# Two interleaved column tiles in the second block's projection, experts adding straight into the stream, and a reordered choice stage

## The reference, cut to what matters

```python
def first_block(x, ...):
    ...                                      # modulation, two attentions, out projection
    h2 = rms_norm(x, g_ffn) * (1.0 + sc_m) + sh_m
    x = x + gt_m * expert_choice_ffn(h2, ...)
    return rms_norm(x, g_final)

def expert_choice_ffn(h, ...):
    aff = softmax(h @ w_router + b_router)
    gate, idx = top_k(transpose(aff), 128)   # 128 tokens for each of 16 experts
    ye = (silu(xe @ w_gate) * (xe @ w_up)) @ w_down      # xe = h[idx]
    return scatter_add(idx, ye * gate)

def second_block(x, ...):                    # twice:
    h  = rms_norm(x, g)  * (1 + sc) + sh     # 1024 tokens; the 256 of the context likewise
    qa, ka, va, ga, qb, kb, vb, gb, qn, kn, vn, gn = split_proj(h @ w_in[l])  # 3584 columns
    ...                                      # q and k: rms norm per head, rotation; 3 attentions
    x = x + gt * (concat([ya, yb, yn]) @ w_out[l])
```

## Time and profile before

| | us |
|---|---|
| median of 3 runs | 4779.21 (4777.91 to 4781.35) |
| the profiled execution | 4777.51 |
| its span in the trace | 4775.8 |
| around the span | 1.7 |

### The profile page before, as it was taken

One profiled execution on the slowest core, in us unless ns is written; L12 is line 12 of the kernel. 1 busy time (PEld: TensorE's weight loads), 2 busy tenths in 40 slices (PEclk: granted clock), 3 DMA queues, 4 the chain that ended last, 5 costly groups with the idle time before them and its releaser, 6 DMA issues. The chain is left out here.

```text
span 4775.8 us, 70956 instructions
## 1 busy us (share of the span) xinstructions
PE 3700.5 (77%) x24823; PEld 3010.7 (63%) x24823; DVE 2445.8 (51%) x4503; ACT 2213.4 (46%) x3911; POOL 914.9 (19%) x756
## 2 busy tenths in 40 slices
PE   3986786887369999378987869675878987869548
PEld 3974665666258888266776647554657776658436
DVE  2114454443468878576425535465585425546555
ACT  2215554751047777322226657554332226657452
POOL 0214000000026565044540000000034540000002
PEclk7988998998679999689998989897989999989889
DMA  6237413414969999422323242332222323232432
GB/s 247 77 111 229 98 41 75 107 41 161 275 252 392 398 394 363 138 71 84 102 79 74 79 89 58 82 93 73 95 88 71 105 91 73 80 78 59 99 99 85
DMA packets 328019, 633.36 MB, mean 133 GB/s; under 512 B 115172, under 2 KB 171396, under 8 KB 326628
## 3 DMA queue, kind: packets, MB, share of 16 engines
q1 hardware_dynamic: 292448, 510.46, 34.1%
q0 software_dynamic: 33760, 112.88, 7.6%
q10 hardware_dynamic: 1444, 5.30, 0.3%
HBM read 490.39 MB, written 138.17 MB: 132 GB/s over the span
## 5 line engine op out<-in xcount | busy, mean ns | idle before, releaser
L1932 PE MATMUL pr_ps<-pr_wH,hT_part 128*128 128x512 f32 (+1 forms) x1120 | 438.8, 392 | 0.0
L1692 ACT ACTIVATE ex_high<-ex_ring 128x2048 fp32r<-128x2048 f32 x192 | 368.7, 1920 | 95.2 <-PE ex_pg L1668 39.9
L1738 DVE TENSOR_TENSOR ex_ring_part<-ex_ring,ex_high 128x2048 fp32r<-128x2048 f32 x144 | 371.8, 2582 | 49.9 <-ACTq L1693 37.9
L1932 PE MATMUL pr_ps<-pr_wH,x_sb_part 128*128 128x512 f32 x896 | 368.5, 411 | 10.4 <-DVEq L2006 10.4
L1932 PE MATMUL pr_ps<-pr_ws_part,x_sb_part 128*128 128x512 f32 x896 | 360.3, 402 | 0.0
L1145 DVE TENSOR_REDUCE aa_nm<-aa_ps 128x1 f32<-128x1280 f32 (+1 forms) x144 | 197.7, 1373 | 303.4 <-PE aa_ps L1051 302.7
L1633 POOL TENSOR_TENSOR ex_ring_part<-ex_ring,ex_high 128x2048 fp32r<-128x2048 f32 x48 | 238.4, 4966 | 216.9 <-ACTq L1693 216.9
L1061 PE MATMUL aa_ps<-ident,aa_prob 128*128 128x128 f32 x1312 | 209.8, 294 | 59.9 <-ACTq L1181 58.6
L1177 ACT ACTIVATE aa_prob<-aa_ps,aa_nm 128x512 f32<-128x512 f32 (+2 forms) x272 | 210.9, 775 | 87.5 <-DVEq L1146 45.3
L1932 PEld LDWEIGHTS pr_ps<-pr_wH,hT_part 128*128 128x128 f32 x1120 | 219.3, 196 | 46.4
L1145 DVE TENSOR_REDUCE ab_nm<-ab_ps 128x1 f32<-128x1280 f32 (+1 forms) x108 | 148.3, 1373 | 194.5 <-PE ab_ps L1051 194.1
(11 more groups left out here) (364 smaller groups left out, 9202.4 us busy)
## 6 DMA issues: line engine op xcount, KB each, us to landing
ex_ring<-in_w_gate SPq DMA_DIRECT2D x64, 1024.0 KB, 9.7
ex_ring<-in_w_up SPq DMA_DIRECT2D x64, 1024.0 KB, 8.1
ex_ring<-in_w_down SPq DMA_DIRECT2D x64, 1024.0 KB, 7.9
z_d<-pr_zT POOLq DMA_DIRECT2D x120, 256.0 KB, 3.1
pr_ws<-in_w_in SPq DMA_DIRECT2D x14, 2048.0 KB, 9.3
mod_w<-in_w_ada SPq DMA_DIRECT2D x10, 2048.0 KB, 13.4
rt_mw<-in_w_ada SPq DMA_DIRECT2D x8, 2048.0 KB, 13.1
proj<-pr_raw POOLq DMA_DIRECT2D x54, 256.0 KB, 2.3
```

The costliest lines, as they stand in the source:

```text
L1692: scalar.activation(wH[:, c % HL].bitcast(F32R), w_sb[:, c % SL], ACT.Copy)
L1738: vector.tensor_tensor(w_part[:, c % SL].bitcast(F32R), w_sb[:, c % SL], wH[:, c % HL], ALU.subtract)
L1932: mm = tensor.matmul(ps[:, g % 4, c0:c1], x.bitcast(F32R), w[:, c % 2, kk, c0:c1].bitcast(F32R), start=kk == 0 and i == 0, stop=kk == KC - ...
```

## The change

It has six parts:

1. **Projection.** The column tiles are taken in the order 1, 0, 3, 2, 6, 4, 5, and two neighbours of that order alternate: the second half of the token tiles of one (`SHIFT` = 5) between the first half of the next. `LAG` goes from 2 to 3, the weight ring from 2 to 3 slots, the rings `raw` and `zT` shrink to 2. The gain is taken with one or two broadcast instructions instead of one over a stored row, and DVE takes the sums and the rest of one step one after the other.
2. **Norm.** The first three column tiles are loaded ahead, not two.
3. **Router.** `x_d` is written in the grid's order, with a DRAM pattern of 2 by 64 rows; `moe_d` and its zeros are gone.
4. **Choice.** The 8 reordering loads are gone; the 11 expert loads are issued as 4, 4 and 3, each group ahead of one of the last three modulation chunks.
5. **Experts and close.** The gate vector is loaded at the experts' start and multiplied in with L1762's successor; the DMA adds to `x_d`. The close stage loads `x_d` in 8 transfers, has no multiplication and addition, and works in two halves with a root each.
6. **Output, second block.** All 8 pieces of the weights are split first (`W0` = `KC`).

```diff
-            W0 = 2
+            W0 = KC if make_y else 2
...
-                    pool.dma_start(x_d[t * P:(t + 1) * P, :], x_sb[:, t * D:(t + 1) * D]).then_inc(kept, 16)
-                    pool.dma_start(moe_d[t * P:(t + 1) * P, :], zero[:, :]).then_inc(zeroed, 16)
+                    pool.dma_start(x_d.rearrange("(c r) d -> r c d", r=ROWS)[t * P // GRID:(t + 1) * P // GRID],
+                                   x_sb[:, t * D:(t + 1) * D]).then_inc(kept, 16)
...
-                for ci in range(TC):
-                    sp.dma_start(x_sb[ci * ROWS:(ci + 1) * ROWS, :].rearrange("p (t d) -> p t d", d=D), by_columns(x_d)[ci])\
-                        .then_inc(turned, 16)
+                def experts(c0, c1):
+                    for c, (m, e, s_) in list(enumerate(expert_chunks()))[c0:c1]:
+                        sp.dma_start(ring[:, c], expert_rows(m, e, s_)).then_inc(wl[c], 16)
...
-                    if i == MW:
-                        for c, (m, e, s_) in enumerate(expert_chunks()[0:EX_RING]):
-                            sp.dma_start(ring[:, c], expert_rows(m, e, s_)).then_inc(wl[c], 16)
                     if i >= MW:
+                        experts((i - MW) * 4, min((i - MW + 1) * 4, EX_RING))
                         sp.wait_ge(mod_ps, i - MW + 1)
...
-                    pool.indirect_dma_start(moe_d, bass.IndirectOffsetOnAxis(ap=to_c[:, e:e + 1], axis=0), y[:, :], None,
+                    pool.indirect_dma_start(x_d, bass.IndirectOffsetOnAxis(ap=to_c[:, e:e + 1], axis=0), y[:, :], None,
...
-                    vector.tensor_scalar(y[:, :], pd[:, :], gate_c[:, e:e + 1], None, ALU.mult)
+                    else:
+                        dve.wait_ge(gl, 16)
+                    vector.scalar_tensor_tensor(y[:, :], pd[:, :], gate_c[:, e:e + 1], gt, ALU.mult, ALU.mult)
...
+                for t in range(ST):
+                    sp.dma_start(x_sb[:, t * D:(t + 1) * D], x_d[t * P:(t + 1) * P, :]).then_inc(xl[t], 16)
...
-        N, LAG, RAW, ZR = 512, 2, 4, 3
+        N, LAG, RAW, ZR, WS = 512, 3, 2, 2, 3
...
-        steps = [(c, t) for c in tiles_c for t in range(ST2)]
+        places = [(0, t) for t in range(SHIFT)]
+        for i in range(NC):
+            for t in range(SHIFT, ST2):
+                places += [(i, t)] + ([(i + 1, t - SHIFT)] if i + 1 < NC else [])
+        steps = [(order[i], t) for i, t in places]
+        begin = [places.index((i, 0)) for i in range(NC)]
+        end = [places.index((i, ST2 - 1)) for i in range(NC)]
+
+        split_after = {}
+        for i in range(1, NC):
+            for kk in range(KC):
+                split_after.setdefault(max(begin[i] - KC - 1 + kk, 0), []).append((i, kk))
...
-                    vector.tensor_tensor(zq, zq, gain[:, ZC[c]:ZC[c] + w], ALU.mult)
+                    for m, (at, cs, _, _) in enumerate(gains):
+                        h0, h1 = (max(at, ZC[c]) - ZC[c]) // hd, (min(at + cs, ZC[c] + w) - ZC[c]) // hd
+                        if h0 < h1:
+                            vector.tensor_tensor(z3[:, h0:h1, :], z3[:, h0:h1, :],
+                                                 g1[:, m:m + 1, 0:hd].to_broadcast([P, h1 - h0, hd]), ALU.mult)
...
-                for q in range(len(qk) + 1):
...
+                for g in qk:
+                    sums(g)
+                    rest(g)
```

More of the change, by code:

```diff
@@ L1805, in _, with summed @@
             def _(act):
+                def summed(x, out_):
+                    scalar.activation(sqr[:, :], x, ACT.Square, accum_out=out_)
+                    act.drain()
                 for t in range(CT):
[L1807 to L1812, removed]
@@ L1813, in _ @@
-                act.drain().then_inc(sq, 1)
-                act.wait_ge(var, 1)
-                scalar.activation(rt[:, :], ss[:, :], ACT.Sqrt)
-                act.drain().then_inc(root, 1)
+                    summed(ctx_sb[:, t * D:(t + 1) * D], squares[:, ST + t:ST + t + 1])
+                for i, (t0, t1) in enumerate(halves_):
+                    for t in range(t0, t1):
+                        act.wait_ge(xl[t], 16)
+                        summed(x_sb[:, t * D:(t + 1) * D], ss[:, t:t + 1])
+                    act.drain().then_inc(sq, 1)
+                    act.wait_ge(var, i + 1)
+                    scalar.activation(rt[:, t0:t1], ss[:, t0:t1], ACT.Sqrt)
+                    act.drain().then_inc(root, 1)
@@ L1928, in _ @@
                             if t == 0:
[L1929 removed]
+                                pe.wait_ge(w_low if i else w_first, (i - 1) * KC + kk + 1 if i else kk + 1)
                             hH, hL = high_of(t)[:, kk * P:(kk + 1) * P], hT_part[:, kk, t * P:(t + 1) * P]
[L1931 to L1933 removed]
+                            for m, (x, w) in enumerate(((hH, wH), (hH, w_part), (hL, wH))):
+                                mm = tensor.matmul(ps[:, g % 4, c0:c1], x.bitcast(F32R), w[:, i % WS, kk, c0:c1].bitcast(F32R),
+                                                   start=kk == 0 and m == 0, stop=kk == KC - 1 and m == 2)
                         mm.then_inc(mm_done, 1)
@@ L1988, in _ @@
                         turned(g - LAG)
-                    if g < len(steps) and c + 1 < len(tiles_c) and 1 <= t <= KC:
-                        weights_high(c + 1, t - 1)
+                    for i, kk in split_after.get(g, ()):
+                        weights_high(i, kk)
             @block.vector
@@ L2007, in _ @@
                 dve.wait_ge(gl, 16 * 7)
-                for m, (at, cs, nm_, w) in enumerate(gains):
-                    scale = w ** -0.5 if "_q_" in nm_ else 1.0
-                    vector.tensor_scalar(gain[:, at:at + cs].rearrange("p (h d) -> p h d", d=w),
-                                         g1[:, m:m + 1, 0:w].to_broadcast([P, cs // w, w]), scale, None, ALU.mult)
+                for m, (_, _, nm_, w) in enumerate(gains):
+                    if "_q_" in nm_:
+                        vector.tensor_scalar(g1[:, m, 0:w], g1[:, m, 0:w], w ** -0.5, None, ALU.mult)
                 dve.drain()
@@ L2179, in first_block @@
             hT, hT_part = twins(held, "hT1", [P, KC, S])
-            ring, ahead = weight_ring(held, "p1", a["w_in"][0], IN1 // 6)
+            ring, ahead = weight_ring(held, "p1", a["w_in"][0], IN1 // 6, (0, 1))
             stage_norm("n1", [(x_sb, ST, 0, D, 0)], a["g_mix"], hT, ahead=ahead)
@@ L2241, in second_layer @@
             hT, hT_part = twins(held, f"hT2{l}", [P, KC, S2])
-            ring, ahead = weight_ring(held, f"pr{l}", a["w_in_2"][l], 512)
+            ring, ahead = weight_ring(held, f"pr{l}", a["w_in_2"][l], 512, COLUMN_TILES[0:3])
             stage_norm(f"n2{l}", [(x_sb, ST, 1, base + D, base), (ctx_sb, CT, 2, base + D, base)],
```

117 lines of the change are left out of this document (47 added, 70 removed).

## The result

The kernel after takes 4670.3 us in the median (4669.1 to 4670.9); before it was 4779.4. The ratio is 0.977 (95% interval 0.975 to 0.979): 109 us faster. Forecast were 4642.5, with 4570 to 4685 as the range. A stage is counted from the first instruction of its list to the first of the next one's; choice and experts begin here with their first working instruction, the first `max` and the first gather. The unchanged stages ahead of the router took 1.7 less in this execution; in the kernels of this study the router starts anywhere from 1137.0 to 1149.4.

A forecast was written before the change was run, and what follows sets the result against it. No engine bounds the whole; each stage ends by its own last arrival. Projection -120, norm +9, choice -44, router +50, close -15, output -15 make -135 against 4777.5: 4642.5 us, range 4570 to 4685.

The forecast's parts named there:

- Router: Router stage: dropping the zeros gains 5, but the reordered store to x_d costs more; 50 us more in sum (25 to 67).
- the upper bound: Router's x_d store: cut by its outermost count, two DMA engines carry 256 KB each, 10.5 us.
- The plain-store rival: Router: the reordered store costs no more than the plain one; -5 instead of +50, 4587.5 in all; chance 0.27.
- Projection, pace: Projection, first matmul to last step at PE's pace: 406 and 374 us, 60 and 78 less in layers 0 and 1.
- the 2.4 us that a pair leaves: Projection: DVE's slack in a pair of heavy and raw step, some 11.5 us on PE against DVE's 9.08.
- the hold on DVE and its price, 2.0: Projection: POOL's weight pieces may block DVE on a shared port pair; 2.0 again makes 11.1 of 11.5, the sum stays.
- 14.3 us a step: Projection: slower case, holds lengthen DVE's heavy step; decides from 14.3 us on; at 15.6, 4838 in all; chance 0.03.
- Projection, end: Projection, after the last step: half is queries and keys with a longer chain behind; some 8 us a layer more (5 to 11).
- the ring of 2: Projection: the rings of 2 come round after two heavy steps, 23 us.
- Choice: Choice stage: eight loads go, DVE's waits of 46.3 us shrink to some 2; 44 less (30 to 46).
- Close, norm, output: Close 15 less (8 to 18); norm stages 9 more (4 to 11); output 15 less (10 to 18).
- The rival of half the projection's gain: Projection: POOL and DVE get in each other's way, so only 60 of the gain comes; 4702.5 in all; chance 0.08.

The follow-up runs named there:

- the run with eight instructions more: Kernel after with 8 more 128x256 DVE instructions in each of the 40 heavy query and key steps: 4793.4 us, 0.35% slower than the kernel before.
- with SP issuing: Kernel after with all projection stores issued by SP instead of POOL: 4648.3 us; the same with 4 more DVE instructions in each heavy step: 4669.4 us.
- a dose of 2.0: Kernel after with 4 more 128x256 DVE instructions in each of the 40 heavy query and key steps: 4717.0 us.

## Why the prediction was right, and where it was off

**What held.** The shape of it, stage by stage: the loss in the router against the gains elsewhere, and the sum's sign and most of its size. Of 135 us forecast 107.6 came; the 27 that are missing are 12 from the router, 10 from the projections, 3 from the choice, 4 from the experts and 3 from the attentions, with some 4 back from the stages ahead of the router, the output and the close.

- **Router.** The mechanism was right, the upper bound was the one to take. Off was the rate: the sum took 25 GB/s for an engine; alone, two engines moved 44, 22 each. The steps were 17.0, not 15.9, which is 8.2 over seven of them. The end was as forecast: from the last issue to the choice it takes 8.7 more than before. The sum had also taken off 5 for the zeros; ahead of the first store 1.2 came of it. That is the 12 us, inside the bound of 67. The plain-store rival (4587.5) fell.
- **Projection, pace.** 406 and 374 forecast from first matmul to last step, 403.2 and 376.1 measured. But the cover was told too large. Of "the 2.4 us that a pair leaves" 0.8 could be used in the mean, and nothing is left in the half-wide pairs of layer 1. The prediction had named the hold on DVE and its price, 2.0, and that the sum would stand with 11.1 of 11.5: the heavy step above took 11.3 of 11.47. And it had named 14.3 us a step as the point from which the kernel gets slower; in the run with eight instructions more most heavy steps follow each other at 14.2 to 15.3 us, and it is slower than before by 0.35%. What it did not have is the share of the distance, some 18 us, which it had only as a margin.
- **Projection, end.** This step failed in size: +8 a layer, bounds 5 and 11, measured +14.4 and +15.0. The chain was counted (sums, root, Newton, transposes, split, stores) for one step; after the last step POOL had four query and key steps queued behind each other, 3.0 each, and ACT waited 4.1 and 2.6 for landed stores, since the ring of 2, which the prediction called covered, isn't covered in this place. 13.4 of the 27 us are here.
- **Choice.** 5.4 us of wait instead of 2. The 24.1 MB were reckoned at 400 GB/s and 60 us; the last chunk was in 64.4 us into the stage, which is 374 GB/s, and its product was there at 68.0.
- **Experts, attentions.** Nothing was forecast, 3.6 and 3.1 came; kernels with the same stages lie as far apart, so these are not put to the change; the experts' stage is the longer one where PE's full clock comes later.
- **Close, norm, output.** -15.9, +9.5 and -16.7 against -15, +9 and -15. First product 34.6 and 34.2 us after the start of the output stage, as forecast (34).

The rival of half the projection's gain had its cause right and its effect wrong: POOL and DVE do get in each other's way, but mostly inside the slack; in layer 1 the pace was some 5 us better with SP issuing.

## What to carry to other kernels

When a store's order is changed, look at what its DRAM side counts first: here one instruction more (two halves of 64) gave back 65 us in its stage, all that one store of two rows of the grid had cost. When one engine's work is spread so that it fits under another's, put extra work on it and see at what dose the time moves; the rows showed 2.4 us of room where a dose of 2.0 already cost 1.2. And when a stage ends with the steps that have the longest tail, count the tail for all that are queued, not for one.

## What the runs showed of the hardware

- A store of 512 KB from GpSimd's queue whose DRAM side counts 2 and then 64 occupied 2.2 of 16 DMA engines and moved 44 GB/s; the same rows in two stores that count 64 landed in 5.6 us instead of 14.4.
- In the projections of the kernel after, DVE's `tensor_tensor` of 128x256 usually take 0.43 us; the 19 `tensor_tensor` that lasted 1.95 us or more all started while POOL issued a store with a POOL `tensor_tensor` of 1.3 us directly behind it. The 71 that started in an issue with no computing instruction directly behind were not held. With SP issuing, 2.0 us more work a heavy step cost 0.5 us in layer 0 instead of 16.5.
- In the second 25 us of the experts' stage the granted clock of PE was 1.00 in five kernels and 0.86 or 0.93 in nine; the stage took 589.2 to 589.9 us in the five and up to 593.7 in the others.
